# Six modulation rows: from TensorE products to running sums on VectorE and GpSimd

## The reference, cut to what matters

```python
mod_ctx = (jax.nn.silu(c_ctx) @ w_mod[l] + b_mod[l])[None, None, :]
mod_lat = (jax.nn.silu(c) @ w_mod[l] + b_mod[l])[:, None, :]
...
shift1, scale1, gate1, shift2, scale2, gate2 = jnp.split(mod, 6, axis=-1)
h = rms_norm(x, g_attn) * (1.0 + scale1) + shift1
m, own_ctx = token_mixing(h, mix_w, rope, ctx, lam_init)
x = x + gate1 * m
h = rms_norm(x, g_ffn) * (1.0 + scale2) + shift2
x = x + gate2 * expert_choice_ffn(h, *moe_w)
```

## Time and profile before

| what | value |
|---|---|
| median of 3 runs | 1145.85 us |
| the profiled execution's own time | 1145.81 us |
| its span, first to last instruction | 1144.0 us |
| TensorE busy | 1097.6 us, 96% of the span |
| VectorE busy | 528.1 us, 46% |
| ScalarE busy | 363.2 us, 32% |
| GpSimd busy | 132.4 us, 12% |
| mean granted TensorE clock | 0.992 of full |
| products 6 to 14 | 355 to 581 us |
| expert products | from 619.4 us |

### The profile page before, as it was taken

How to read it: one execution, slowest core, us unless ns; L and a number is a source line. 1 busy time by engine, 2 the same in 40 slices (tenths; PEclk the granted TensorE clock), 3 DMA queues, 4 the chain that set the end, 5 groups by cost and what they waited for, 6 DMA issues and landing times.

```text
span 1144.0 us, 28118 instructions
## 1 busy us (share of the span) xinstructions
PE 1097.6 (96%) x12524; PEld 828.2 (72%) x12524; DVE 528.1 (46%) x961; ACT 363.2 (32%) x846; POOL 132.4 (12%) x173
## 2 busy tenths in 40 slices
PE   6999999999999999999998999999999999999993
PEld 4679875666677777777877877777777777777761
DVE  4574538879958142334976033332233223333235
ACT  4333327778753223022163221222222222211103
POOL 2332300000000000002012111111110111110021
PEclk9999999999999999999999999999999999999997
DMA  9932242111031545359987999999999999999993
GB/s 359 299 107 68 77 84 63 35 31 41 1 109 38 184 147 147 106 190 300 355 303 320 402 398 406 407 405 409 414 406 405 408 404 408 405 408 405 410 321 143
DMA packets 86747, 295.32 MB, mean 258 GB/s; under 512 B 27249, under 2 KB 28530, under 8 KB 62050
## 3 DMA queue, kind: packets, MB, share of 16 engines
q1 hardware_dynamic: 79104, 269.77, 61.5%
q0 software_dynamic: 6528, 20.10, 6.1%
q10 hardware_dynamic: 994, 3.65, 0.9%
HBM read 273.25 MB, written 15.00 MB: 252 GB/s over the span
## 4 chain that ended last, share of the span: by engine, by line
PE 85%; DMA 7%; issue 2%; ACT 2%; DVE 2%; SPq 1%; POOLq 0%; POOL 0%; ACTq 0%; DVEq 0%
PE ps L1207 39%; PE ps L772 10%; PE ps L774 9%; PE ps L773 9%; PE ps L994 4%; PE ps L1013 3%; PE ps L1032 2%; PE ps L1036 2%; DMA x_dram<-y_row,rows_t 2%; DMA x_dram<-xn_p 1%; DMA raw_first<-in_w_in_dram 1%; DMA x_f<-x_dram 1%; PE ps L794 1%; DMA raw<-in_w_in_dram 1%; PE ps L978 1%
## 5 line engine op out<-in xcount | busy, mean ns | idle before, releaser
L2124 DVE SCALAR_TENSOR_TENSOR y_row<-ps,gates,gate_q 32x256 f32<-32x256 f32 (+1 forms) x184 | 88.3, 480 | 238.5 <-PE ps L1207 236.0
L1564 ACT ACTIVATE h_t<-ps 128x256 f32<-128x256 f32 x48 | 15.0, 384 | 374.7 <-PE ps L1207 374.7
L772 PE MATMUL ps<-w_hi,ht 128*128 128x512 f32 (+1 forms) x320 | 124.2, 388 | 0.6 <-DVE q_n L1728 0.6
L774 PE MATMUL ps<-w_hi,ht 128*128 128x512 f32 (+1 forms) x320 | 121.8, 381 | 0.0
L773 PE MATMUL ps<-raw_lo,ht 128*128 128x512 f32 (+1 forms) x320 | 121.7, 380 | 0.0
L1207 PE MATMUL ps<-late,xe 128*32 128x256 f32 x1824 | 103.6, 379 | 0.0
L537 DVE TENSOR_TENSOR raw_lo<-raw,w_hi 128x1024 fp32r<-128x1024 f32 x48 | 58.2, 1234 | 78.9 <-ACT w_hi L532 78.2
L1207 PEld LDWEIGHTS ps<-late,xe 128*32 128x32 f32 x1824 | 77.0, 110 | 23.3
L1207 PE MATMUL ps<-raw,xe 128*32 128x256 f32 x1392 | 88.1, 379 | 0.9 <-issue 0.8
L532 ACT ACTIVATE w_hi<-raw 128x1024 fp32r<-128x1024 f32 x48 | 48.7, 1053 | 123.6 <-DMA raw<-in_w_in_dram 68.1
L2354 POOL DMA_INDIRECT xg<-x_dram,rows x48 | 46.1, 961 | 320.7 <-PE ps L1207 293.2
(11 more groups left out here) (315 smaller groups left out, 1831.0 us busy)
## 6 DMA issues: line engine op xcount, KB each, us to landing
late<-in_w_exp_down_dram SPq DMA_DIRECT2D x25, 1024.0 KB, 20.4
late<-in_w_exp_up_dram SPq DMA_DIRECT2D x21, 1024.0 KB, 28.8
late<-in_w_exp_gate_dram SPq DMA_DIRECT2D x17, 1024.0 KB, 24.7
raw<-in_w_in_dram SPq DMA_DIRECT2D x16, 1024.0 KB, 5.5
raw<-in_w_exp_gate_dram SPq DMA_DIRECT2D x16, 1024.0 KB
raw_gate<-in_w_exp_up_dram SPq DMA_DIRECT2D x14, 1024.0 KB
raw<-in_w_exp_up_dram SPq DMA_DIRECT2D x13, 1024.0 KB
raw_gate<-in_w_exp_down_dram SPq DMA_DIRECT2D x13, 1024.0 KB
```

The source lines that it names most:

```text
L772: pe.matmul(b, stat_hi(k, tt), hi[:, kk, :], start=first, stop=False)
L774: mm = pe.matmul(b, stat_lo(k, tt), hi[:, kk, :], start=False, stop=last)
L2124: return dve.scalar_tensor_tensor(y_row[n % 2][32 * v:32 * v + count, 256 * q:256 * q + 256], bank(b, o, o + 256, src), gates[src, n % EG, ...
```

## The change

TensorE no longer multiplies the twelve modulation chunks. VectorE sums condition 0 and GpSimd condition 1, block by block: each block's elements times a per-partition scalar, added to a running sum of 128 x 512. The sum over the 128 partitions is left to the turn or spread, whose fixed operand is now 1/128 everywhere; c_s holds the conditions times 128. The chunks stand one behind each product chunk from product 6 to 13, rows 6 to 9 first and then 4 and 5. VectorE's four steps of a chunk stand at (j, 2q, 2), (j, 2q, 4), (j, 2q+1, 1) and (j, 2q+1, 3); GpSimd works chunk by chunk, and its DMAs for gate1, x_r and the router weights stand before chunk (5, 0). A modulation chunk's place is free when both engines have used it. The tiles of rows 6, 7 and 4 are the same, so row 7 waits for turn 6 and row 4 for turn 7. The turns, the spreads and two waits for the first expert loads are moved.

```diff
-MODS_AFTER = {(6, 0): [(4, 0), (4, 1)], (7, 0): [(5, 0)], (7, 1): [(5, 1)], (8, 0): [(6, 0)], (9, 0): [(6, 1)],
-              (9, 1): [(7, 0)], (10, 0): [(7, 1)], (11, 0): [(8, 0), (8, 1)], (11, 1): [(9, 0)], (12, 0): [(9, 1)],
-              }
+MODS_AFTER = {(6, 0): [(6, 0)], (7, 0): [(6, 1)], (7, 1): [(7, 0)], (8, 0): [(7, 1)], (9, 0): [(8, 0)], (9, 1): [(8, 1)],
+              (10, 0): [(9, 0)], (11, 0): [(9, 1)], (11, 1): [(4, 0)], (12, 0): [(4, 1)], (13, 0): [(5, 0)], (13, 1): [(5, 1)]}
+MOD_CHUNKS = [_e for _l in MODS_AFTER.values() for _e in _l]
...
-TURNS = {(9, 1, 0): ("merged", 0), (9, 1, 2): ("merged", 1), (9, 1, 4): ("merged", 2), (9, 2, 1): ("merged", 3),
-         (9, 2, 3): ("merged", 4), (10, 0, 2): ("turn", 6), (11, 0, 2): ("turn", 7), (12, 0, 2): ("turn", 8),
-         (12, 0, 4): ("spread", 4, 0), (12, 1, 1): ("spread", 4, 1), (12, 1, 3): ("spread", 5, 0),
-         (13, 0, 0): ("spread", 5, 1), (13, 0, 2): ("turn", 9), (13, 0, 3): ("merged", 5), (13, 0, 4): ("merged", 6),
-         (13, 1, 0): ("merged", 7), (13, 1, 1): ("merged", 8), (13, 1, 3): ("merged", 9),
-         (14, 1, 2): ("bias", 0)}
+TURNS = {(7, 3, 3): ("turn", 6), (9, 1, 0): ("merged", 0), (9, 1, 2): ("merged", 1), (9, 1, 4): ("merged", 2),
+         (9, 2, 1): ("merged", 3), (9, 2, 3): ("merged", 4), (9, 2, 4): ("turn", 7), (11, 0, 3): ("turn", 8),
+         (12, 0, 2): ("turn", 9), (13, 0, 3): ("merged", 5), (13, 0, 4): ("merged", 6), (13, 1, 0): ("merged", 7),
+         (13, 1, 1): ("merged", 8), (13, 1, 3): ("merged", 9), (13, 2, 1): ("spread", 4, 0), (13, 2, 3): ("spread", 4, 1),
+         (14, 0, 2): ("spread", 5, 0), (14, 0, 4): ("spread", 5, 1), (14, 1, 2): ("bias", 0)}
+POSITIONS = [(_j, _h, _t) for _j in range(6, 15) for _h in range(2 * chunks_of(_j)) for _t in range(NT)]
+MOD_STEPS = {}
+for (_j, _q), _l in MODS_AFTER.items():
+    _o = POSITIONS.index((_j, 2 * _q, 2))
+    for _i, _s in enumerate((_n, _r, _g) for _n, _r in _l for _g in range(4)):
+        MOD_STEPS.setdefault(POSITIONS[_o + 2 * _i], []).append(_s)
...
-        mod_keep = at("mod_keep", 143360, [P, 2, NW])
+        mod_acc = [at("mod_acc0", 143360, [P, 2, NW]), at("mod_acc1", 112640, [P, 2, NW]), at("mod_acc2", 116736, [P, 2, NW]),
+                   at("mod_acc3", 122880, [P, 2, NW])]
+        mod_tmp = [at("mod_tmp0", 133120, [P, NW]), at("mod_tmp1", 120832, [P, NW]), at("mod_tmp2", 126976, [P, NW])]
...
+        def acc_of(n):
+            return mod_acc[{6: 0, 7: 0, 8: 1, 9: 2, 4: 0, 5: 3}[n]]
+        def acc_free(eng, n):
+            user = {7: 6, 4: 7}.get(n)
+            if user:
+                eng.wait_ge(s_post, MOD_COUNT["turn", user])
+        def mod_done(n):
+            return 4 * (MOD_CHUNKS.index((n, 1)) + 1)
...
+                    if STREAM[last_use][0] == "mod":
+                        use = 4 * (MOD_CHUNKS.index(STREAM[last_use][1:]) + 1)
+                        sp.wait_ge(s_modd, use)
+                        sp.wait_ge(s_modp, use)
+                    else:
+                        sp.wait_ge(s_half, 2 * last_use + 2)
...
-                        sp.wait_ge(s_half, gemm_half(13, 1) + 1)
+                        sp.wait_ge(s_half, gemm_half(13, 3) + 1)
                     elif c == 3:
-                        sp.wait_ge(s_half, gemm_half(13, 3) + 1)
+                        sp.wait_ge(s_modd, mod_done(5))
+                        sp.wait_ge(s_modp, mod_done(5))
...
-                    if hh % 2 == 1:
-                        for m, q in MODS_AFTER.get((j, hh // 2), []):
-                            mod_chunk(m, q)
-            def mod_chunk(n, q):
-                if q == 0:
-                    pe.wait_ge(s_row, n)
-                    if n == 4:
-                        pe.wait_ge(s_yme, 2 * HB)
-                chunk = CHUNK["mod", n, q]
-                pe.wait_ge(s_raw[chunk % NRAW], raw_count[chunk])
-                for g in range(4):
-                    k = 4 * q + g
-                    mm = pe.matmul(bank(7, rows=slice(32 * g, 32 * g + 2)), c_t[:, k, :],
-                                   raw[:, chunk % NRAW, g * NW:(g + 1) * NW], start=(q == 0), stop=(q == 1))
-                mm.then_inc(s_half, 2)
...
-                pe.wait_ge(s_row, n + 1)
+                o = T_MEAN - T_KEPT
                 if event[0] == "turn":
+                    pe.wait_ge(s_modd, mod_done(n))
+                    pe.wait_ge(s_modp, mod_done(n))
                     for i in range(4):
-                        mm = pe.matmul(bank(6, 2 * i, 2 * i + 2), row_of(n)[:, i * P:(i + 1) * P],
-                                       tab2[:, T_SELM - T_KEPT:T_SELM - T_KEPT + 2], start=True, stop=True)
+                        for v in range(2):
+                            mm = pe.matmul(bank(6, 2 * i + v, 2 * i + v + 1), acc_of(n)[:, v, i * P:(i + 1) * P],
+                                           tab2[:, o:o + 1], start=True, stop=True)
                 else:
-                    o = T_SB - T_KEPT + event[2] * P
-                    mm = pe.matmul(bank(6), tab2[:, o:o + P], row_of(n), start=True, stop=True)
+                    pe.wait_ge(s_modp if event[2] else s_modd, mod_done(n))
+                    mm = pe.matmul(bank(6), tab2[:, o:o + P], acc_of(n)[:, event[2], :], start=True, stop=True)
...
+            dve.tensor_scalar(c_s[:, :, :], c_t, float(P), None, ALU.mult).then_inc(s_dve, 1)
...
+                if n == NT:
+                    dve.wait_ge(s_modp, mod_done(4))
...
+            def mod_step(n, q, g):
+                k = 4 * q + g
+                chunk = CHUNK["mod", n, q]
+                if g == 0:
+                    dve.wait_ge(s_raw[chunk % NRAW], raw_count[chunk])
+                w, c, acc = raw[:, chunk % NRAW, g * NW:(g + 1) * NW], c_s[:, k, 0:1], acc_of(n)[:, 0, :]
+                if k == 0:
+                    acc_free(dve, n)
+                    dve.tensor_scalar(acc, w, c, None, ALU.mult).then_inc(s_modd, 1)
+                else:
+                    dve.wait_ge(s_modd, 4 * MOD_CHUNKS.index((n, q)) + g)
+                    dve.scalar_tensor_tensor(acc, w, c, acc, ALU.mult, ALU.add).then_inc(s_modd, 1)
...
+                        for step in MOD_STEPS.get((j, hh, t), []):
+                            mod_step(*step)
...
+            def mod_chunk(n, q):
+                chunk = CHUNK["mod", n, q]
+                acc, tmp = acc_of(n)[:, 1, :], mod_tmp[{6: 0, 7: 0, 5: 2}.get(n, 1)][:, :]
+                if q == 0:
+                    acc_free(pool, n)
+                    if n == 6:
+                        pool.wait_ge(s_yl, 8)
+                    if n in (8, 5):
+                        pool.wait_ge(s_mrg, NT if n == 8 else 2 * NT)
+                pool.wait_ge(s_raw[chunk % NRAW], raw_count[chunk])
+                for g in range(4):
+                    k = 4 * q + g
+                    w, c = raw[:, chunk % NRAW, g * NW:(g + 1) * NW], c_s[:, k, 1:2]
+                    if k == 0:
+                        pool.tensor_scalar(acc, w, c, one, ALU.mult, ALU.mult).then_inc(s_modp, 1)
+                    else:
+                        pool.wait_ge(s_modp, 4 * MOD_CHUNKS.index((n, q)) + g)
+                        pool.tensor_scalar(tmp, w, c, one, ALU.mult, ALU.mult).then_inc(s_pool, 1)
+                        pool.wait_ge(s_pool, own())
+                        pool.tensor_tensor(acc, acc, tmp, ALU.add).then_inc(s_modp, 1)
+            for n, q in MOD_CHUNKS:
+                if (n, q) == (5, 0):
+                    pool.wait_ge(s_half, gemm_half(11, 3) + 1)
+                    for v in range(2):
+                        pool.dma_start(gate1[:, v, :], b_mod[:, 2 * D:3 * D].to_broadcast([P, D])).then_inc(s_gb, 16)
+                    pool.wait_ge(s_half, gemm_half(12, 1) + 1)
+                    pool.dma_start(x_r[:, 0:NTL, :], x_sample[0].rearrange("(t p) d -> p t d", p=P)).then_inc(s_xr, 16)
+                    pool.dma_start(x_r[:, NTL, :], x_prompt[0]).then_inc(s_xr, 16)
+                    pool.dma_start(router[:, :, :], w_router[0].rearrange("(k p) e -> p k e", p=P)).then_inc(s_router, 16)
+                mod_chunk(n, q)
```

More of the change, by code:

```diff
@@ L252, in build @@
         scale2 = sb("scale2", [P, KD, 2])
+        c_s = sb("c_s", [P, KD, 2])
         mods_q = sb("mods_q", [P, KD, 4])
@@ L416, in build @@
         s_xta = sem("s_xta"); s_xtd = sem("s_xtd")
-        s_row = sem("s_row"); s_post = sem("s_post"); s_mod = sem("s_mod"); s_scale = sem("s_scale")
+        s_row = sem("s_row"); s_modd = sem("s_modd"); s_modp = sem("s_modp"); s_post = sem("s_post"); s_mod = sem("s_mod"); s_scale = sem("s_scale")
         s_ss = sem("s_ss"); s_rs = sem("s_rs"); s_xn = sem("s_xn"); s_xt = sem("s_xt")
@@ L776, in product @@
                             mm.then_inc(s_acc, 1)
-                    mm.then_inc(s_half, 1)
+                    mm.then_inc(s_half, 1 + 2 * len(MODS_AFTER.get((j, hh // 2), []) if hh % 2 else []))
                     if after_half:
                         after_half(hh)
-                    if hh % 2 == 1:
```

(37 more changed lines are left out.)

6 lines of the change are left out of this document (removed).

## The result

The changed kernel takes 1149.03 us in the median of 11 runs (1147.26 to 1153.44), the kernel before 1145.5 beside it: a ratio of 1.0040 (95% interval 1.0025 to 1.0054). A second set of six runs gave 1.0030 (1.0016 to 1.0043). So it is slower by 0.3 to 0.4%, some 4 us, where I had forecast no change. The eleven runs fall into a lower group (six, 1147.26 to 1149.03 us) and an upper one (five, 1151.14 to 1153.44).

A forecast was written before the change was run, and what follows sets the result against it. TensorE, holding 85% of the chain, was taken to bound the kernel. Against 1145.81 us: -13.3 + 3.3 + 5.7 + 2.3 + 1.4 + 0.3 = -0.3, so 1145.5; own range 1143 to 1148.5, 8-in-10 range 1138.5 to 1150.5.

The forecast's parts named there:

- chunks off TensorE: TensorE, products 6 to 14: removing eight single modulation chunks and two pairs saves 13.3 us.
- four turns: TensorE, turns of rows 6 to 9: eight one-column matmuls replace four two-column ones, +3.3 us (bounds +2.4 and +3.6).
- wait at turn 7: Turn 7 at (9,2,4): TensorE waits for merged 4's low part, +5.7 us (bounds 4.2 and 6.3).
- wait at merged 6: Product 13: its later second weight load delays merged 5's low part, so TensorE waits +2.3 us (bounds 1.0 and 5.0).
- wait at merged 1 (contention): GpSimd beside VectorE lengthens two splits, in the chains of the two new stalls: +0.3 us in sum.
- wait at the bias (loads): Gate, product 14 and first expert loads, issued together, are caught up before product 14 ends: 0 us.
- clock, as the remainder: Granted clock falls in the idle at turn 7: +1.4 us (bounds 0 and 2.5); merged 6 an even chance, left out.
- The third rival: Both new chains: contended splits and additions wait out whole GpSimd instructions, clock also falls at merged 6: 1148.4 us; chance 0.10.
- The first of my rivals: Stalls at turn 7 and merged 6 absent or small: 1135.8 us without any, 1140 with half; chance 0.22.
- GpSimd: 9 us a chunk: GpSimd's multiplications and additions take about 9 us a modulation chunk (bounds 6 and 12.5), so it keeps up.
- the rival of a late GpSimd: GpSimd can't keep up from 398 us; at 15 us a chunk row 4 is 8 us late for merged 5: 1151; chance 0.13.

The follow-up runs named there:

- profiled run: The traced execution of the changed kernel, no further edit: 1153.44 us, the slowest of the upper group.
- the run of 1147.96 us: Also called the lower run: a later trace of the changed kernel, no further edit, from the lower group: 1147.96 us.
- the earlier trace: Profiled run of the kernel before, which the prediction read: 1145.81 us.
- The last experiment: Changed kernel with turn 7 later, merged 5 and 6 earlier, gate loads behind product 14's second chunk, row 8's VectorE sums later: 1135.85 us, ratio 0.9918 to the kernel before.
- The exchange of the loads: Changed kernel with the four gate chunks' loads issued behind product 14's second chunk instead of ahead: 1148.27 us, ratio 1.0019 to the kernel before.

## Why the prediction was wrong

The account at the mark, in us, for the profiled run and the run of 1147.96 us:

| step | predicted | profiled run | lower run |
|---|---|---|---|
| chunks off TensorE | -13.3 | -13.3 | -13.3 |
| four turns | +3.3 | +3.6 | +3.6 |
| wait at turn 7 | +5.7 | +4.3 | +4.3 |
| wait at merged 6 | +2.3 | +2.3 | +2.3 |
| wait at merged 1 (contention) | +0.3 | +1.2 | +1.2 |
| wait at the bias (loads) | 0 | +2.8 | +1.2 |
| wait at spread (5,1) | 0 | +0.4 | +0.4 |
| ahead of product 6 | 0 | -1.1 | -1.2 |
| clock, as the remainder | +1.4 | +7.5 | +5.6 |
| at the mark | -0.3 | +7.7 | +4.1 |

The granted clock bears the remainder out. By it (0.68 in 436 to 452 us, 0.79 in 524 to 532, 0.86 in 560 to 572) TensorE was at its lower level for 10.2 us at turn 7 and 3.4 each at merged 6 and the bias in the profiled run, 2.2 of them in idle; half of the other 14.8 is 7.4. In the lower run it was 6.8 and 3.4 us: 5.1, which leaves 0.5 unexplained. The 1.1 us ahead of product 6 come from the idle of the earlier trace rows: TensorE waits 2.75 us there in the kernel before, and the clock falls; in the changed kernel it waits 1.67 us (0.9 in the lower run) at 49.2, and the clock does not fall in any of the twelve traces of it and its variants. With one trace of the kernel before, whether the change or that run makes this difference stays open.

Behind the mark the lower run is 2.0 us shorter than the kernel before, so its time is only 2.15 us above that kernel's profiled run. The range of the prediction held the time, in part by luck: turn 7's wait came out 1.4 us shorter and product 6 starts 1.1 earlier than forecast, which hid part of what the other terms lacked. What was wrong is that the losses about cancel the gain. The step of the prediction that failed is its term for the clock, 1.4 us where the runs show 5.6 to 7.5, and beside it the loads of product 14, put at nothing where the bias waits 1.2 to 2.8 us. The third rival, at 1148.4 us, lay nearest to the measured 1149.03. The fall of the clock at merged 6 came as it said; its price for the lock in the two chains did not, and the loads were not in it, so that it is near is luck too.

- **Chunks and turns: right.** No product of a modulation chunk is left on TensorE. A turn costs 397.09 - 394.83 - 0.467 = 1.79, 0.89 more than the earlier trace rows, so the upper bound held (and by my own figures the four turns are 3.2, not 3.3): a record of one column costs as much as one of two. The last experiment, where nearly all waits are gone, lands within 0.1 us of these two terms and the waits left.
- **Turn 7: right in its mechanism, 1.4 too long.** Its chain is that of the earlier trace rows. The load is issued 0.43 us after the start of the half's last matmul (430.34), as there (0.42), but lands sooner, and the modulation load is issued only at 432.75, behind it: that is the case which the prediction priced at its lower bound, 4.2.

```profile
430.77 1.31 SPq L688 DMA_DIRECT2D raw<-in_w_branch_a_dram  x2
...
437.95 1.06 ACT L539 ACTIVATE w_hi<-raw 128x1024 fp32r<-128x1024 f32 x1 [4.73 <-DMA raw<-in_w_branch_a_dram]
...
439.04 1.81 DVE L544 TENSOR_TENSOR raw_lo<-raw,w_hi 128x1024 fp32r<-128x1024 f32 x1 [3.50 <-ACT w_hi L539]
440.77 0.68 DVE L1891 TENSOR_TENSOR mt_lo<-ps,mt_hi 128x512 fp32r<-128x512 f32 x1
```

  From issue to ScalarE it is 7.2 us here and 9.1 in the earlier trace rows; the longer split (1.81 for 1.23) takes 0.6 of that back. The first of my rivals, that the stalls don't form, is refuted.
- **Merged 6: right**, 2.33 for 2.3. The load is issued at 515.47 us, ScalarE splits it at 520.44, and merged 5's low part is done at 523.74, in the order that the prediction has.
- **The clock: the term that failed most.** I took the 1.4 us of the earlier trace rows and left merged 6 to an even chance outside the sum. Turn 7 alone takes 3.3 to 3.4 instead of 1.7 us, and behind it 3.7 to 5 us of products run at half speed: 3.4 to 4.2 us lost. The earlier trace rows showed a recovery 2.9 us after TensorE had work again; here the clock stood at its lower level for 6.8 us (lower run) to 10.2 us (profiled run). An idle stretch followed by eight products of one column is not the case that the earlier trace rows shows, and my upper bound of 2.5 was no bound. At merged 6, which I left out, the clock fell in all four traces of the changed kernel. The experiments bear it out: with TensorE busy in the waits about 2 us go, although 3.4 us of slow clock remain; without turn 7's wait 8 us go for 4.3 of wait.
- **"Loads: 0": wrong.** The bytes were right (21 us estimated, 21.8 from issue to split), the point in time they were held against was not. I asked that they be there before product 14 ends; its second chunk is split at (14,0,2), in order ahead of the gate's additions, which free bank 6 for the bias. In the kernel before, the same issue came at 519.73 and was split at 547.30. The exchange of the loads showed it: the split comes at 543 us, and the bias waits for nothing.
- **Contention: 0.3 for 1.2.** The price for each instruction was about right (the split 1.81 instead of 1.23 in turn 7's chain), but I looked for it in the two chains with a stall and not where VectorE has the most to do, at merged 0 and 1. The wait there is the longer steps and their place together: it goes without GpSimd's sums, and it goes with row 8's steps moved. By the Trainium skill (SBUF — State Buffer, "SBUF: two separate sides") a VectorE instruction with two SBUF inputs waits for the whole of a GpSimd instruction that holds their shared port pair. The runs agree that VectorE's steps lengthen beside GpSimd (1042 against 746 ns) and that those which read PSUM do not (L1891 at 685 and 688). The step at 426.25 takes 1.77 us, 1.0 more than the mean without GpSimd's sums; over all steps the surcharge is 0.3 us in the mean against GpSimd's 1.2 to 1.5, so a step waits on average for much less than a whole instruction.
- **GpSimd: 9 us a chunk, measured about 11**, inside the bounds. It has this many instructions and this mean length in 360 to 575 us:

```profile
L2334 POOL TENSOR_TENSOR mod_acc<-mod_acc,mod_tmp 128x512 f32<-128x512 f32 x42 | 63.2, 1505 | 3.5
L2332 POOL TENSOR_SCALAR mod_tmp<-raw,c_s,tab 128x512 f32<-128x512 f32 x42 | 49.3, 1173 | 21.6 <-DMA raw<-in_w_mod_dram 17.4 <-POOL mod_acc L2334 0.5
```

  It is never the last releaser of TensorE, so the rival of a late GpSimd is out. It was the last to free the place for five modulation loads (22.7 us of SyncE's waits, up to 8.6), which I had not expected; no load of a product waited for it.
